# Mixed attention, RWKV and expert blocks on one core: the first pair of experts begins between two parts of its gather

## The reference

```python
MOE_GROUPS, MOE_EPG, MOE_EXPERTS, MOE_TOPK, MOE_HIDDEN = 4, 8, 32, 2, 512

def hier_moe(x, rg_w, rg_b, re_w, re_b, w_gu, w_down):
    g_prob = softmax(t @ rg_w + rg_b)            # t: the 256 tokens
    g_p, g_idx = top_k(g_prob, 1)
    e_logits = (t @ re_w + re_b) of the chosen group
    e_p, e_idx = top_k(softmax(e_logits), MOE_TOPK)
    gate = g_p * e_p / sum(e_p)
    ...
    def expert_block(args):                      # the tokens xb of expert e
        hg, hu = jnp.split(xb @ w_gu[e], 2, axis=-1)
        return (jax.nn.silu(hg) * hu) @ w_down[e]
    ...
    out = segment_sum(y * gate, token)
```

## Time and profile before

| what | value |
|---|---|
| median of 3 runs | 1991.49 us (1991.07 to 1996.47) |
| the profiled execution | 1995.43 us, span 1993.6 us |
| mean granted TensorE clock | 0.929 |
| TensorE busy | 83% of the span |
| DMA engines busy | 64.8% of the span for the weight queue |
| weight tiles of the expert layers | 192 transfers of 2048 KB |

### The profile page before, as it was taken

The page is one execution under the profiler, slowest core; times in us unless marked ns, Lnnn a source line. Parts: engine busy times, 40 slices in busy tenths (PEclk is TensorE's granted clock), DMA queues, the critical chain, the costliest instruction groups (busy, mean ns, idle before and its releaser), DMA issues.

```text
span 1993.6 us, 30675 instructions
## 1 busy us (share of the span) xinstructions
PE 1651.8 (83%) x13266; PEld 1046.2 (52%) x13266; DVE 654.3 (33%) x1153; ACT 371.0 (19%) x739; POOL 190.7 (10%) x91
## 2 busy tenths in 40 slices
PE   9999999999999997766566897999887767766664
PEld 6998976998986754222122332767854223221211
DVE  1355431355431464111111123573365212111103
ACT  1344211444201341000000011331211000000001
POOL 2231322231320000000000000000300000000000
PEclk9999999999999997988998898999997989888887
DMA  9342444342444456999999997222155999999994
GB/s 376 106 161 102 153 156 169 100 166 86 165 194 184 173 211 254 426 427 426 427 426 428 425 395 284 85 85 77 56 234 220 426 429 424 426 429 425 429 426 187
DMA packets 48230, 537.14 MB, mean 269 GB/s; under 512 B 4532, under 2 KB 12980, under 8 KB 15032
## 3 DMA queue, kind: packets, MB, share of 16 engines
q1 hardware_dynamic: 46752, 528.27, 64.8%
q10 hardware_dynamic: 1304, 6.51, 0.8%
HBM read 533.71 MB, written 1.05 MB: 268 GB/s over the span
## 4 chain that ended last, share of the span: by engine, by line
PE 58%; DMA 33%; DVE 5%; ACT 2%; issue 1%; POOL 0%; DVEq 0%; ACTq 0%; POOLq 0%
PE ps L447 48%; DMA arena<-in_moe_w_gu 27%; PE ps L459 7%; DMA ring<-in_moe_w_gu 5%; PE ps L465 3%; ACT arena L2379 1%; DVE x L1512 1%; DVE arena L1512 1%; DVE arena L1501 1%; ACT arena L2383 0%; PE ps L454 0%; DVE small L1506 0%; DVE small L1535 0%; DVE hb L1501 0%; ACT L2379 0%
## 5 line engine op out<-in xcount | busy, mean ns | idle before, releaser
L459 PE MATMUL ps<-arena 128*32 128x512 f32 (+1 forms) x1348 | 205.7, 692 | 85.4 <-DMA arena<-in_moe_w_gu 63.9
L2383 ACT ACTIVATE arena<-ps 128x512 f32<-128x512 f32 (+4 forms) x150 | 95.3, 636 | 899.1 <-PE ps L459 501.5
L459 PE MATMUL ps<-ring,arena 128*32 128x512 f32 x1248 | 176.7, 697 | 92.3 <-DMA ring<-in_moe_w_gu 71.6
L1501 DVE TENSOR_TENSOR arena<-arena,ps 128x256 f32<-128x256 f32 (+2 forms) x106 | 52.9, 499 | 495.0 <-ACT arena L2379 440.7
L447 PE MATMUL ps<-hT,ring 128*128 128x256 f32 (+2 forms) x1280 | 208.5, 322 | 0.2 <-DVE arena L1512 0.2
L447 PEld LDWEIGHTS ps<-hT,ring 128*128 128x128 f32 (+1 forms) x1280 | 184.9, 185 | 20.2 <-issue 1.8
L447 PE MATMUL ps<-arena 64*64 64x64 f32 (+8 forms) x2080 | 161.6, 295 | 28.6 <-ACT arena L2677 22.2
L459 PEld LDWEIGHTS ps<-arena 128*32 128x32 f32 (+1 forms) x1348 | 49.4, 126 | 225.0 <-DMA arena<-in_moe_w_gu 98.1
L447 PEld LDWEIGHTS ps<-arena 64*64 64x64 f32 (+3 forms) x2080 | 109.3, 154 | 78.1 <-ACT arena L2677 49.4
L459 PEld LDWEIGHTS ps<-ring,arena 128*32 128x32 f32 x1248 | 38.1, 119 | 207.2 <-DMA ring<-in_moe_w_gu 101.7
L447 PE MATMUL ps<-ring,hT 128*128 128x256 f32 (+3 forms) x512 | 140.5, 432 | 0.9 <-DVE hT L1524 0.9
(11 more groups left out here) (199 smaller groups left out, 1788.3 us busy)
## 6 DMA issues: line engine op xcount, KB each, us to landing
arena<-in_moe_w_gu SPq DMA_DIRECT2D x57, 2048.0 KB, 41.9
ring<-in_moe_w_gu SPq DMA_DIRECT2D x49, 2048.0 KB, 41.4
ring<-in_moe_w_down SPq DMA_DIRECT2D x35, 2048.0 KB, 41.4
arena<-in_moe_w_down SPq DMA_DIRECT2D x29, 2048.0 KB, 41.3
extra<-in_moe_w_gu SPq DMA_DIRECT2D x22, 2048.0 KB, 41.5
ring<-in_w_merge SPq DMA_DIRECT2D x16, 2048.0 KB, 8.5
ring<-in_w_in SPq DMA_DIRECT2D x9, 2048.0 KB, 7.4
ring<-in_attn_w_qkv SPq DMA_DIRECT2D x6, 2048.0 KB, 7.2
```

The costliest lines, as they stand in the source:

```text
L459: i = t.matmul(o, l, r, start=first, stop=last, skip_group_check=True)
L1501: v.tensor_tensor(o, a, b, op).then_inc(*dve.one(name))
L2383: s.activation(o, a, ACT.Copy).then_inc(*act.one(name))
```

## The change

There are four edits in the head of the expert stages, the same for both layers.

1. TensorE gathers only chunks 0 to 3 ahead of the branch, as two quarters of two chunks, into two different PSUM banks. Behind the branch, in `first_round` of pair 0, it multiplies `gu0` and `gu1` first, then gathers chunks 4 to 7 and transposes the gates (`rest_of_first`), then multiplies `gu2` and `gu3`.
2. ScalarE copies the two quarters one by one (`first xe0`, `first xe1`), 256 columns each, in place of one copy of 512. `gu0` waits for the first, `gu1` for the second, `gu2` for VectorE's copy of the second half.
3. VectorE computes the flag `few` right behind the count, ahead of the other flags. TensorE waits for `few` alone before it loads it. On the rare path it still waits for all flags.
4. Two semaphores of their own (`first_gathered`, `first_turned`) tell VectorE and ScalarE of the second half of the gather and of the transposes.

```diff
+    m.first_gathered, m.first_turned = sem("first_gathered"), sem("first_turned")
...
+        def rest_of_first():
+
+            for n, (o, a, b, first, last) in enumerate(gathered(psum[0][:, 512:1024], range(4, 8))):
+                i = t.matmul(o, a, b, start=first, stop=last, skip_group_check=True)
+                if n == 7:
+                    i.then_inc(m.first_gathered, 1)
+            t.wait_ge(*dve(M + "0 places"))
+            for n, (o, a, b) in enumerate(gates_T(psum[1][:, 0:512])):
+                i = t.transpose(o, a, b)
+                if n == 3:
+                    i.then_inc(m.first_turned, 1)
+            t.wait_ge(*dve(M + "first xe"))
...
             xp = e.xe[pr // 2 % 2].rearrange("p (k e n) -> p k e n", k=KT, e=4)
+            if pr == 0 and q == 2:
+                rest_of_first()
+            elif pr == 0 and q < 2:
+                t.wait_ge(*act(M + f"first xe{q}"))
             t.wait_ge(*m.w.landed(M + f"{pr} gu{q}"))
...
         t.wait_ge(*dve(M + "0 oh"))
-        for half in range(2):
-            gather(psum[0][:, 512 * half:512 * half + 512], half, M + f"first gather{half}")
-        t.wait_ge(*dve(M + "0 places"))
-        gates_T(psum[1][:, 0:512], M + "first gatesT")
+        for quarter, buf in enumerate((psum[0][:, 0:256], psum[1][:, 512:768])):
+            mm(gathered(buf, range(2 * quarter, 2 * quarter + 2)), M + f"first gather{quarter}")
...
             if pr == 0:
-                t.wait_ge(*dve(M + "flags"))
+                t.wait_ge(*dve(M + "few"))
                 few = t.value_load(e.few[0:1, 0:1], min_val=0, max_val=1)
...
             red(cnt, p[:, 64:96].rearrange("p (q a) -> p q a", a=2), MAX, M + "count")
+            ts(cnt2, cnt, CAP + 0.5, None, ALU.is_lt, None)
+            cp(e.few, cnt2, M + "few")
             ts(cnt2, cnt, 3 * CAP + 0.5, None, ALU.is_gt, None)
             cp(e.flag2, cnt2)
...
-            ts(cnt2, cnt, CAP + 0.5, None, ALU.is_lt, None)
-            cp(e.few, cnt2)
             ts(cnt, cnt, CAP + 0.5, None, ALU.is_gt, None)
             cp(e.flag, cnt, M + "flags")
...
-        v.wait_ge(*pe(M + "first gather1"))
+        v.wait_ge(m.first_gathered, l + 1)
         cp(e.xe[0][:, 512:1024], psum[0][:, 512:1024], M + "first xe")
-        v.wait_ge(*pe(M + "first gatesT"))
+        v.wait_ge(m.first_turned, l + 1)
         places(1)
...
-        s.wait_ge(*pe(M + "first gather0"))
-        cp(e.xe[0][:, 0:512], psum[0][:, 0:512])
-        s.wait_ge(*pe(M + "first gatesT"))
+        for quarter, buf in enumerate((psum[0][:, 0:256], psum[1][:, 512:768])):
+            s.wait_ge(*pe(M + f"first gather{quarter}"))
+            cp(e.xe[0][:, 256 * quarter:256 * quarter + 256], buf, M + f"first xe{quarter}")
+        s.wait_ge(m.first_turned, l + 1)
         cp(e.ogT[0], psum[1][:, 0:512])
```

26 lines of the change are left out of this document (12 added, 14 removed).

## The result

The changed kernel takes 1982.06 us (median of 5 runs, 1979.67 to 1983.73); the kernel before takes 1991.49 us (5 runs, 1991.07 to 1996.47). The ratio is 0.9935, with a 95% interval from 0.9922 to 0.9949: faster by 0.65%, 13 us by the ratio and 9.4 us by the medians. The two differ because the five runs of the kernel before fall into three of 1991.1 to 1991.5 us and two of 1995.6 and 1996.5 us, and their median is one of the lower three. Predicted were 7.0 us, with 1983.0 us as the lower end. The time lies 0.9 us under the range. The profiled execution took 1979.67 us with a span of 1977.9.

The account below looks back on a forecast made before the run. The transfer queue, full from each stage's first refill, was taken to bound the kernel. First refills 3.1 and 3.9 us earlier sum to 7.0 us, taken off the median 1991.49: 1984.5 us, range 1983.0 to 1989.5 us.

Parts of the forecast that it names:

- What bounds the kernel: Both expert stages: transfer queue full from the first refill, so each stage ends a fixed time behind it, 430.0 us in layer two.
- The flag: Head of the stages: `few` ready at 767.64 us, before TensorE comes to it, so it costs nothing.
- The branch and the run ahead: Ahead of `gu0`: instruction issue runs ahead during the gather and covers flag loads and branch; `gu0` at 770.5 and 1527.0 us.
- the gather in front of it: Ahead of `gu0`: 0.207 us a record; sixteen of 32 leave the path, so TensorE's array is free at 770.36 us.
- The rival of an uncovered branch: Ahead of `gu0`: branch not covered, `gu0` at 771.5 and 1528.0 us, gain 5.6 us; within the partial gain's chance of 0.33.
- The clock: Both heads: rise stays 5.9 and 3.7 us into the gather, so first refills come 3.1 and 3.9 us earlier.
- a late rise: Both heads, rival: clock stays low through `gu0`, gain 2.6 + 2.3 = 4.9 us; within the partial gain's chance of 0.33.
- the partial gain: Both heads, rival: branch uncovered, clock low through `gu0`, or both; typically 5.2 us, 1986.3 us; chance 0.33.
- The moved work: Between `gu1` and `gu2`: late gather costs nothing; refill 3 at 780.0 us, queue dry only at 783.4, 3.4 us of slack.
- The code's place: Pair 0's branch, rival: a 2.50 us instruction-supply stop in both heads, leaving 2.0 us, 1989.5 us; chance 0.04.
- the chain is right: Up to 810.56 us, rival: the pairs' work decides, not the queue; pair 0's end moves 0.2 us, 1991.5 us; chance 0.08.
- slower: Behind refill 2, rival: third refill too late, queue runs dry, 4.0 us lost in each layer, 1999.5 us; chance 0.05.

Follow-up runs that it names:

- e4: Changed kernel with the first refill of each expert stage made to wait for `gu1` in place of `gu0`: 1983.52 us, ratio 0.9950.
- e6: Kernel before with only the flag order changed, `few` computed first and TensorE waiting for it alone: 1994.59 us, ratio 1.0003.
- e12: Changed kernel with six unread multiplications ahead of the counting products and only a quarter of the gather ahead of `gu0`: 1981.66 us, ratio 0.9941.
- e15: Changed kernel, unchanged, run again on one chip with others: 1981.53 us, ratio 0.9933 to the kernel before.
- e2: Changed kernel with 113 and 115 transposes in pair 0's never executed block, moving later rare blocks: 1981.51 us, ratio 0.9941.
- e14: Kernel before with 23 never executed transposes, moving later rare blocks 46 instructions as the change does: 1989.30 us, ratio 0.9973.
- e13: Changed kernel with 105 never executed transposes, putting later rare blocks 256 instructions behind those of the kernel before: 1987.48 us, ratio 0.9969.
- e5: Kernel before, unchanged, run once more for a second trace: 1993.25 us, ratio 1.0001.
- e9: Kernel before with 128 never executed transposes in the first layer, moving later rare blocks by 256 instructions: 1994.40 us, ratio 1.0007.
- e10: Kernel before with 5 never executed transposes in the first layer, moving later rare blocks by 10 instructions: 1993.39 us, ratio 0.9996.
- e7: Changed kernel with nine unread multiplications in TensorE's idle time ahead of the counting products, rare blocks moved by padding: 1979.66 us, ratio 0.9922.
- e11: Changed kernel with six unread multiplications in TensorE's idle time ahead of the counting products, rare blocks moved by padding: 1976.72 us, ratio 0.9921.
- e16: Changed kernel with six unread multiplications ahead of the counting products, run a second time: 1975.90 us, ratio 0.9914.

## Why the prediction was wrong

**What bounds the kernel: right.** Full DMA engines from the first refill, and a fixed distance behind it: 339.0 to 340.3 us to the takeover in 18 traces with first refills from 4.6 to 9.7 us behind the gather, and 429.7 to 430.1 us to the last `gu3` of the second layer. e4 shows it with the refill alone moved. One sum beside it is off: by the order of issue the last `gu3` is the 85th refill and not the 87th, so 430.0 us are 5.06 us a tile and not 4.91. The forecast took the distance from the trace and not from this sum. From the takeover to pair 13's last product it is less fixed: 56.4 us in four traces, 57.6 to 59.2 us in the others, by the granted clock; that adds to the scatter and not to the gain.

**The flag: right**, at nothing (e6).

**The branch and the run ahead: right; the gather in front of it mis-sized by 0.3 us.** `gu0` was to start 3.45 us behind the gather and started at 3.7 us. TensorE's multiplications have no gap there, its weight loads one of 0.22 us. What is longer is the gather: 0.207 us a record was the mean over 6.62 us of which the last 0.75 ran at the upper clock. At the lower level a record takes (5.87 + 2 x 0.75) / 32 = 0.23 us, and sixteen take 3.7 us, as measured. The rival of an uncovered branch (4.5 us) did not come. e12 shows the gap where the gather is too short to cover it: 1.44 us.

**The clock: the first failed step, -1.1 us.** I left the rise where the kernel before had it, at 5.9 and 3.7 us behind the gather's start. In the changed kernel it came at some 6.0 us in the first layer and 5.8 in the second, so the second `gu0` took 2.92 us and not 2.05. That term was 3.9 us and measured 2.7; the first was 3.1 and measured 2.9. Sum 5.6 for 7.0 us. Of the 1.4 us the longer gather has 0.3: with `gu0` at the measured 3.7 us and the rises where I had left them, the refills would have come at 6.7 and 5.7 us, a gain of 3.0 + 3.7 us. The other 1.1 us are the late rise, 1.0 of it in the second head. I named a late rise as a rival ("the rise came 2.2 us apart in the two heads, so it can come later") and gave the partial gain 5.2 us. That rival is the one that happened in the heads, and in the second one alone. e15 had the rise earlier in its first head (5.53 us), so the term is itself a matter of the execution.

**The moved work: right.** Refill 3 came 13.2 us behind the gather (13 predicted), the queue never dry.

**The code's place: the step that was left out, +5.2 us.** This step put the time below the range. I read the stop at pair 14, and used it only as something that might come to pair 0. Against it I wrote that "the layout of code changes by a few instructions only". It changes by 46 instructions for every later rare block, and 16 were enough to take the stop away (e2). I took its being where it was for granted, and priced only its coming, not its going. Since TensorE is the limit at pair 14, its 2.5 us and the half clock behind it (5.2 us together) are on the path in full. e14 and e13 show this from both sides.

**The baseline:** I took 7.0 us off the median 1991.49 of three runs. On the other chips or at other times before had 1993.6 to 1994.3 us (14 to 23 runs), so those three were at its lower side, which hid some 2 us of the gain.

**Luck.** That the median came within 0.9 us of the range is luck: 5.2 us left out on one side, 1.4 us too much in the heads and some 2 us of a low baseline on the other. The range was right for the heads, whose 5.6 us alone would have given 1985.9 us, and it did not hold the second mechanism at all.

The other rivals: "the chain is right" and "slower" did not come, as the third refill and e4 show.

## What to carry to other kernels

Where a queue of transfers is full from its first issue to the end of a stage, as here, the stage moves with that first issue; work may be piled behind it as long as the next issues come before the queue is dry. A stop of 2 to 3 us marked "issue" inside a block behind a branch can hang on where the code lies, as at pair 14: an edit that changes the number of instructions ahead made and removed it, so a gain or loss of that size should be tested by padding a block that never runs before it is put down to the edit. And work moved forward into a stretch of low clock becomes slower there (`gu0` 2.8 to 3.6 us in place of 1.9 in most of the changed heads): cost it at the clock of its new place, or give the engine unread work in the idle time ahead.

## What the runs showed of the hardware

The stop at pair 14 is an edge in the code. It stays when the blocks move by 256 instructions and comes 4 records sooner when they move by 10; the fetches of instructions in the trace have 16384 bytes each, as the queue's line in the page says of 115 packets (kernel before; 114 in its second trace, e5) and of 113 (changed kernel):

```profile
q8 instruction: 115, 1.88, 0.4%
```

```profile
q8 instruction: 113, 1.85, 0.4%
```

In the kernel before one such fetch falls between 1178 and 1181 us (the queues' packets, MB and share of the 16 engines' time in these 3 us; 2.1% of 48 us are 1.0 us):

```profile
q8 instruction: 1, 0.02, 2.1%
```

It starts at 1178.98 us, just when TensorE runs out of work (1179.09 us), and TensorE goes on at 1181.59. The start alone proves nothing, for e14, with the same work and no stop, has a fetch at the same point (1178.62 us, 2.6 us behind its block's start, 2.7 in the kernel before). What differs is the next one: 1185.44 us in the kernel before, 1191.38 in e14. The code with the stop needs one fetch more in this stretch, as an edge inside the block would have it. The Trainium skill, "Runtime: NRT & Kernel Launch", section "Instruction fetch mechanics", gives blocks of 16 KiB and 256 instructions, and calls the cost of crossing such an edge mostly hidden; the size agrees with e9, but 45 instructions behind a taken branch the crossing cost 2.0 to 2.75 us of standing still in six traces (the kernel before, e5, e6, e9, e10, e13; 35 instructions behind it in e10, all by my count). With places from 16 on, where the edge lies at most 29 instructions behind the block's start or ahead of it, there was none at pair 14. Why there is none then was not tried.

The second layer has a stop that this does not explain. It stands ahead of the first record of a block for full experts, in the kernel before and in the changed kernel:

```profile
1648.15 1.92 PE L454 MATMUL ps<-arena 128*32 128x512 f32 x16 [2.51 <-issue]
```

```profile
1633.41 5.57 PE L455 MATMUL ps<-arena 128*32 128x512 f32 x32 [2.43 <-issue]
```

It has 2.4 to 6.4 us in 14 of the 18 traces and is missing in e7, e11, e12 and e16. In five of the traces with it (the kernel before, the changed kernel, e5, e9, e15) a fetch begins 3.4 to 3.5 us ahead of the block's first record. It costs nothing here, for the transfers are the limit there: first refill to last landing is 429.7 to 430.1 us with it and without. What brings it and takes it away was not tried.

A stop of 2.5 us also costs the clock: 0.59 between 1182 and 1185 us behind it, so the price is 5.2 us for 2.5 (4.7 to 5.2 us in the six traces).

TensorE's idle time of 4.1 us ahead of the counting products, filled with six products that nobody reads, brought the clock to its upper level by 765 us in e11 (767 us in e12) and the half gather from 3.78 to 2.05 us. It fell back some 0.3 us into an idle time of 1.44 us behind a short gather (e12, first layer), and not in one of 1.19 us (second layer).
